# Reading order of the constants: positions first, constants without the mask, and the mask behind the first weights

## The reference

```python
def first_block(x, c, positions, rel_bias, norm_gain, w_mod, b_mod, w_in, ...):
    c_act = jax.nn.silu(c)
    for l in range(DEPTH):                       # 2 layers
        mod = c_act @ w_mod[l] + b_mod[l]
        shift, scale, gate = jnp.split(mod, 3, axis=-1)
        h = rmsnorm(x, norm_gain[l]) * (1.0 + scale[:, None, :]) + shift[:, None, :]
        proj = h @ w_in[l]
        ...                                      # split in 11 parts
        att = sparse_attention(...)              # bias = rel_bias[t5_bucket(pos_q - pos_k)]
        ret = retention(rotary(q_b, positions), rotary(k_b, positions) * s, v_b)
        ...
        x = x + gate[:, None, :] * (jnp.concatenate([y_a, y_b], -1) @ w_out[l])
    return x
```

## Time and profile before

| | |
|---|---|
| median of 3 runs | 1845.43 us |
| the profiled execution | 1845.32 us |
| its span, first to last instruction | 1843.5 us |
| PE busy | 98% of the span |
| DVE, ACT, POOL busy | 69%, 52%, 11% |
| DMA, mean over the span | 230 GB/s |
| granted TensorE clock, mean | 0.998 of full |

### The profile page before, as it was taken

One profiled execution on the slowest core, in us unless ns is written; L12 is line 12 of the kernel. 1 busy time (PEld: TensorE's weight loads), 2 busy tenths in 40 slices (PEclk: granted clock), 3 DMA queues, 4 the chain that ended last, 5 costly groups with the idle time before them and its releaser, 6 DMA issues.

```text
span 1843.5 us, 25345 instructions
## 1 busy us (share of the span) xinstructions
PE 1814.4 (98%) x9769; PEld 1478.1 (80%) x9769; DVE 1277.9 (69%) x1779; ACT 963.2 (52%) x1368; POOL 203.0 (11%) x261
## 2 busy tenths in 40 slices
PE   6999999999999999999999999999999999999997
PEld 3568788888888878888988888888888888888886
DVE  6349989998987778658756544488885466665555
ACT  5345565456465446545644644577764445343464
POOL 1000021001000001100000000045440020021001
PEclk9999999999999999999999999999999999999999
DMA  9999879967986976654465565655555555557562
GB/s 357 386 369 353 304 250 334 324 224 231 344 278 231 384 243 222 216 161 151 147 218 184 184 200 187 199 176 167 167 167 198 184 187 178 192 173 261 180 197 92
DMA packets 195155, 424.09 MB, mean 230 GB/s; under 512 B 7392, under 2 KB 12396, under 8 KB 193644
## 3 DMA queue, kind: packets, MB, share of 16 engines
q1 hardware_dynamic: 193228, 414.67, 66.0%
q10 hardware_dynamic: 1824, 8.02, 1.1%
HBM read 418.45 MB, written 4.21 MB: 229 GB/s over the span
## 4 chain that ended last, share of the span: by engine, by line
PE 91%; DVE 4%; DMA 2%; issue 1%; ACT 1%; SPq 0%; DVEq 0%; POOLq 0%; POOL 0%; ACTq 0%
PE acc L770 27%; PE acc L772 26%; PE acc L771 26%; DVE w_lo L2010 1%; DMA raw<-in_w_mod 1%; PE tps L895 1%; PE tps L813 1%; DMA raw<-in_w_in 1%; PE acc L933 1%; PE acc L934 0%; PE acc L935 0%; PE sps L1033 0%; DVE proj L2145 0%; PE sps L1032 0%; DMA proj<-in_positions 0%
## 5 line engine op out<-in xcount | busy, mean ns | idle before, releaser
L2010 DVE TENSOR_TENSOR w_lo<-raw,w_hi 128x1024 fp32r<-128x1024 f32 (+1 forms) x572 | 712.2, 1249 | 449.2 <-ACT w_hi L1386 446.5
L1386 ACT ACTIVATE w_hi<-raw 128x1024 fp32r<-128x1024 f32 (+1 forms) x572 | 599.1, 1051 | 750.0 <-PE acc L772 685.9
L770 PE MATMUL acc<-w_hi,ht_hi 128*128 128x512 f32 (+1 forms) x2272 | 896.9, 395 | 0.8 <-issue 0.8
L772 PE MATMUL acc<-w_hi,ht_lo 128*128 128x512 f32 (+1 forms) x2272 | 881.5, 388 | 0.0
L771 PE MATMUL acc<-w_lo,ht_hi 128*128 128x512 f32 (+1 forms) x2272 | 879.6, 387 | 0.0
L772 PEld LDWEIGHTS acc<-w_hi,ht_lo 128*128 128x128 f32 x2272 | 426.5, 188 | 88.8
L770 PEld LDWEIGHTS acc<-w_hi,ht_hi 128*128 128x128 f32 x2272 | 426.8, 188 | 85.8 <-issue 4.3
L771 PEld LDWEIGHTS acc<-w_lo,ht_hi 128*128 128x128 f32 x2272 | 427.3, 188 | 82.2
L2145 DVE SCALAR_TENSOR_TENSOR proj<-raw,vcol,proj 128x1024 f32<-128x1024 f32 x60 | 80.2, 1338 | 3.8
L2145 DVE SCALAR_TENSOR_TENSOR scr<-raw,vcol,scr 128x1024 f32<-128x1024 f32 x60 | 79.0, 1316 | 4.0
L2842 POOL TENSOR_TENSOR scr<-scr 128x128 f32<-128x128 f32 x56 | 31.0, 586 | 156.8 <-DVE scr L2584 156.8
(11 more groups left out here) (331 smaller groups left out, 1481.6 us busy)
## 6 DMA issues: line engine op xcount, KB each, us to landing
raw<-in_w_in SPq DMA_DIRECT2D x203, 1024.0 KB, 5.1
raw<-in_w_mod SPq DMA_DIRECT2D x64, 1024.0 KB, 5.6
raw<-in_w_out SPq DMA_DIRECT2D x32, 1024.0 KB, 5.2
raw<-in_w_mod SPq DMA_DIRECT2D x44, 512.0 KB, 11.3
raw<-in_w_o SPq DMA_DIRECT2D x16, 1024.0 KB, 5.1
raw<-in_w_ple_gate SPq DMA_DIRECT2D x16, 1024.0 KB, 5.1
raw<-in_w_b_out SPq DMA_DIRECT2D x8, 1024.0 KB, 5.1
raw<-in_w_a_out SPq DMA_DIRECT2D x8, 1024.0 KB, 5.1
```

The source lines that it names most:

```text
L770: pe.matmul(o, hi_m, w_hi[:, slot, u, 0:width], start=start, stop=False)
L772: mm = pe.matmul(o, lo_m, w_hi[:, slot, u, 0:width], start=False, stop=stop)
L1386: act.activation(w_hi[:, x % SPL, :, 0:width], raw[:, j, 2 * (x % halves):2 * (x % halves) + 2, 0:width], ACT.Copy).then_inc(hi_ready, 1)
L2010: dve.tensor_tensor(w_lo[:, x % SPL, :, 0:width], raw[:, j, 2 * (x % halves):2 * (x % halves) + 2, 0:width], w_hi[:, x % SPL, :, 0:width]. ...
```

## The change

Three edits. The mask moves to the end of the constants, so that the small columns and the identity (239 columns) lie together. ACT issues the positions first, then the first 239 columns of the constants (119.5 KB), then the rest as before. SP reads the 256 columns of the mask (128 KB, a DMA of its own with the semaphore `s_mask`) behind the last pieces of the front. DVE waits for `s_mask` as well where it waited for `s_const` ahead of the angles.

```diff
 C_ID = 0
-C_MASK = C_ID + P
-C_INV = C_MASK + 2 * P
+C_INV = C_ID + P
...
 C_TH = C_SEL + 2
-C_N = C_TH + SIGNS
+C_MASK = C_TH + SIGNS
+C_N = C_MASK + 2 * P
...
-    k[:, C_TH:C_N] = [-e for e in EDGES[:SIGNS]]
+    k[:, C_TH:C_MASK] = [-e for e in EDGES[:SIGNS]]
...
         s_const = sem("s_const")
+        s_mask = sem("s_mask")
...
             for g in range(FRONT):
                 first_weights(3, g)
+            sp.dma_start(kst[:, C_MASK:C_N], consts[:, C_MASK:C_N]).then_inc(s_mask, 16)
             free.skip(8 * FRONT)
...
             act.sem_inc(ret_taken, 2)
-            act.dma_start(kst[:, :], consts).then_inc(s_const, 16)
             act.dma_start(prow_i, positions.partition_broadcast(P)).then_inc(s_pos, 16)
+            act.dma_start(kst[:, 0:C_MASK], consts[:, 0:C_MASK]).then_inc(s_const, 16)
...
                 if l == 0:
                     dve.wait_ge(s_const, 16)
+                    dve.wait_ge(s_mask, 16)
                     angles()
                     lower_bound()
```

## The result

The changed kernel takes 1848.68 us (median of 22 runs, 1847.38 to 1850.58) against 1845.44 us (22 runs, 1845.17 to 1846.15): a ratio of 1.0017 with a 95% interval of 1.0011 to 1.0023, +3.24 us. That is outside the range of 1843.8 to 1847.1 and on the other side. The profiled execution took 1849.48 us with a span of 1847.7, so it is 4.2 us longer than the profiled one before, an execution from the slower half.

A forecast was written before the change was run, and what follows sets the result against it. The prediction took bytes to bound the front and PE the rest. Fewer bytes gave -0.3 us and all other terms 0, so the median of 1845.43 became 1845.1 us, range 1843.8 to 1847.1.

The forecast's parts named there:

- What bounds the kernel: Front to about 122 us bound by bytes, the rest by PE; time is the last awaited `w_mod` landing plus a fixed rest.
- Part 1, the bytes: First read loses 131072 bytes ahead of the `w_mod` pieces, so later pieces land earlier: gain 0.3 us, between 0 and 0.34.
- Part 2, the landings: ACT's swapped queue: positions land by 5.3 us, constants at 7.5, at most 7.84.
- Part 2, the product behind POOL: DVE's product or subtractions stand behind POOL's identity copy, making `rel` and the buckets 1.5 to 2.0 us later.
- Part 2, the cover: Queued transfers in the front let SP be 2.9 us late before the DMA engines run dry.
- Part 2 comes to 0: The swap on ACT's queue costs 0 us, its 1.5 to 2.0 us of lateness hidden by queued transfers.
- The later chain costs: Rival, chance 0.2: `rel` behind POOL's copy frees homes up to 2.0 us later, queue runs dry; up to 1847.1 us.
- The earlier chain pays: Rival, chance 0.08: DVE runs beside POOL, buckets come 1.3 us earlier and their chain bounds the front; 1843.8 us.
- Parts 3, 4 and 5: Mask's issue on SP's queue, DVE's wait for it at 137.95 us, and its columns' new place: 0 us each.

The follow-up runs named there:

- the mask alone: Changed kernel with the old order on ACT's queue: constants without the mask first, positions second, mask still behind the front; 1845.12 us, ratio 0.9998.
- the early identity: Changed kernel with POOL's identity copy split: two columns per group first, the rest in 8 pieces after DVE's edges; 1845.55 us, ratio 1.0001.
- five more products: Kernel before the change, with DVE's product of positions and identity made five more times; 1846.64 us, ratio 1.0004.
- the early identity and old order: Changed kernel with the old order on ACT's queue, mask behind the front, and POOL's identity copy split; 1845.19 us, ratio 0.9998.
- seven more products: Kernel before the change, with DVE's product of positions and identity made seven more times; 1848.57 us, ratio 1.0016.

## Why the prediction was wrong, by its own steps

- **What bounds the kernel**: right. The 4.22 us by which the last piece that PE waits for is late are the 4.2 us of the span.
- **Part 1, the bytes**: -0.3 forecast, -0.33 and -0.39 us in the two kernels with the mask late and the old order. Right in size, as far as 0.3 us can be told at all. The sign asked for, the piece taken up at about 120.5, came in the second of them (120.46) and not with the mask alone (120.83), so the traces neither carry nor refute the mechanism.
- **Part 2, the landings**: the first step that failed. The constants were put at 7.5, 7.84 at most, and came at 8.65; the positions were put at 5.3 and came at 6.55. A DMA was given the landing of the one that had stood in its place. The positions read one row 128 times, and that is slower by about 1 us and takes the next DMA with it; with 128 rows of their own in that place the constants came at 7.1.
- **Part 2, the product behind POOL**: the mechanism was right and is shown by the early identity. Its size, 1.5 to 2.0 us, was 3.04, and the constants' landing, 1.15 us later than the 7.5 taken, is about the difference to the 2.0. By the rule quoted from the Trainium skill (SBUF — State Buffer, "SBUF: two separate sides") the product had to wait for the whole copy, since POOL was first by 0.04 us; the trace agrees, with 3.83 us.
- **Part 2, the cover**: the second step that failed. 2.9 us were put down as hidden, the least landing of 8.0 us less the 5.1 us of an unhindered piece; the delays by repeated products show about 1. The 5.1 us are a median of the main loop. In the changed kernel, where the queue had just been down to a share of 0.62, a `w_in` piece of the front still took 6.6 us at least, so 8.0 - 6.6 = 1.4 us would have been nearer:

```profile
DMA to landing us min/median/max: 6.6/12.6/13.8
```

- **The two together**: "Part 2 comes to 0" needed both. With the landing alone wrong, 3.04 us at the signs and 3.79 at the second home against a cover of 2.9, the median of 1845.1 would have become 1845.2 to 1846.0. With the cover alone wrong, 1.5 to 2.0 us against 1, it would have become 1845.6 to 1846.1. Both lie inside the range. Together they give 2.0 to 2.8 us, less 0.3 for the bytes, so +1.7 to +2.5; the measured +3.24 is above that too, by a part that stays open.
- **The later chain costs**: this was the rival, with 0.2 and up to 1847.1. It was the case; its price was capped at 2.0 - 0.3 us because the delay was capped at 2.0, and that made the range too narrow. The rival's condition, a delay of more than 2.9 us, was met (3.04), but the kernel with five more products shows that less is enough.
- **The earlier chain pays**: no, as far as it can be told, by the kernel with the early identity and old order.
- **Parts 3, 4 and 5**: 0, as forecast. The mask was issued at 126.55, not before 125, since the whole front was 4.2 us late, and landed 9.6 us later, before DVE asked for it.
- **A reading that was too smooth**: in the 12 stretches from 10 to 130 us PE was said to lose tenths of a us. It loses 1.85 us from 40 to 50, and in the first of them, 10 to 20, it is busy for 7.36 only the earlier trace rows.

## What to carry to other kernels

Ahead of a swap of two small reads at the start, list every engine that wakes on each of them, and whether two of them then start together on VectorE and GpSimd: the copy that ran harmlessly beside a wait may now stand in front of the one product that everyone waits for. When a full queue is said to hide a delay, the cover is counted to the emptiest moment of that queue and with the landing time of such a piece in such a queue; here a delay beyond it came out in full and more. And a delay can be bought for a few repeated instructions: three kernels of that kind give the cover directly. Last, a DMA that is moved to another place in a queue need not take over the landing of the one that stood there: here the one that read a single row 128 times was later, and so was the one behind it.

## What the runs showed of the hardware that was not expected

- A DVE product with two SBUF inputs took 3.83 us instead of 0.43 beside a 3.60 us POOL copy that had started 0.04 us earlier; seven edges took 7.39 instead of 4.12 us.
- 128 reads of one 1 KB row landed in 5.2 to 5.7 us (six traces), 128 rows of their own in 4.3 us (one trace).
- In the profile with seven more products PE waited 2.1 us, until 124.01, for the `w_mod` piece of the table above, and then the granted clock fell to its lower level of 1.2 GHz (0.50 in the table of stretches), with PE at work again. It cost about 1.5 us: the piece waited for was 3.2 us late, the next one 4.8. This execution, 1850.08 us, is the slowest of the 11, 1.5 us above their median, so the loss of clock is not in the +2.99. In the profile of the change PE's longest such wait was 1.4 us, and the clock stayed at 1.00.

```profile
122.00:124.00 2.00, 0.00 (x0) 0.00 (x0) 1.88 (x2) 0.43 (x1) 0.00 (x0) 1.00 1.04 379
124.00:126.00 2.00, 1.99 (x11) 0.98 (x12) 0.00 (x0) 0.00 (x0) 0.00 (x0) 0.82 1.06 389
126.00:128.00 2.00, 2.00 (x6) 1.51 (x6) 0.00 (x0) 0.00 (x0) 0.00 (x0) 0.50 1.05 386
128.00:130.00 2.00, 2.00 (x11) 1.12 (x12) 0.00 (x0) 0.59 (x1) 0.00 (x0) 0.82 1.05 386
```

- The kernels whose lateness is past the cover scatter more. The middle half of the executions lies within 1.1 us for the change and 0.8 to 1.6 us for the others of that kind, against 0.2 to 0.5 us for the kernel before and those within the cover. A full queue that takes up the scatter of its start as well would explain it; that wasn't tested.
